# The front of a two-block network kernel: another order of the first weight chunks, a first projection split by features, and late modulation chunks multiplied on GpSimd

## What is computed

```python
mod = jax.nn.silu(c) @ w_ada[l] + b_ada[l]            # 1024 x 6144
mod_c = jax.nn.silu(c_ctx) @ w_ada[l] + b_ada[l]
sh1, sc1, g1, sh2, sc2, g2 = jnp.split(mod[:, None, :], 6, axis=-1)
sh1c, sc1c, g1c, sh2c, sc2c, g2c = jnp.split(mod_c, 6, axis=-1)
hc = modulate(rmsnorm(ctx, norm1_g[l]), sh1c, sc1c)   # h * (1 + scale) + shift
mix_c, ctx_states = token_mixers(hc, *mixer_params, zero_states, not last)
hx = modulate(rmsnorm(x, norm1_g[l]), sh1, sc1)
mix_x, _ = token_mixers(hx, *mixer_params, ctx_states, True)
x = x + g1 * (mix_x @ w_out[l])
x = x + g2 * conv_glu(modulate(rmsnorm(x, norm2_g[l]), sh2, sc2), *ffn_params, True)
...
proj = h @ w_in                                       # first thing in token_mixers
q, k, v, z_g, a_g, b_g, z_s, x_s, B_s, C_s, dt_s = _split(proj, GDN_SPLITS + SSM_SPLITS)
```

## Time and profile before

| | us |
|---|---|
| three timed runs: median | 2697.16 |
| lowest, highest | 2693.72, 2697.79 |
| profiled execution: span from its first to its last instruction | 2695.4 |
| of it PE busy | 2571.0 |
| stages that the change touches: from the start to the first matmul of the mixers | 345.28 |

### The profile page before, as it was taken

How to read it: one execution, slowest core, us unless ns; L and a number is a source line. 1 busy time by engine, 2 the same in 40 slices (tenths; PEclk the granted TensorE clock), 3 DMA queues, 4 the chain that set the end, 5 groups by cost and what they waited for, 6 DMA issues and landing times. The chain is left out here.

```text
span 2695.4 us, 47072 instructions
## 1 busy us (share of the span) xinstructions
PE 2571.0 (95%) x20752; PEld 2004.3 (74%) x20752; DVE 1278.8 (47%) x1994; ACT 510.2 (19%) x1023; POOL 577.4 (21%) x373
## 2 busy tenths in 40 slices
PE   6999889989999999999999999999999999999998
PEld 4555568855888887764888468888878764888886
DVE  2123234554899944642677454442332474445233
ACT  3222123221111101112465110000010261000001
POOL 0000055510000000201222033344333100443332
PEclk9999999999999999999999999999999999999999
DMA  7123100021222123120000012222222101122210
GB/s 302 67 121 156 63 2 3 3 95 63 94 81 76 67 86 129 47 94 32 35 4 4 33 63 94 77 80 94 94 80 94 63 1 63 63 94 94 84 72 32
DMA packets 17370, 195.34 MB, mean 72 GB/s; under 512 B 1896, under 2 KB 3048, under 8 KB 5392
## 3 DMA queue, kind: packets, MB, share of 16 engines
q1 hardware_dynamic: 17168, 192.34, 19.0%
HBM read 190.22 MB, written 2.12 MB: 71 GB/s over the span
## 5 line engine op out<-in xcount | busy, mean ns | idle before, releaser
L3462 PE MATMUL psum<-arena,weight_ring 128*128 128x256 f32 x3072 | 671.2, 379 | 2.9 <-ACT arena L3352 2.9
L3462 PEld LDWEIGHTS psum<-arena,weight_ring 128*128 128x128 f32 x3072 | 582.7, 190 | 85.8 <-ACT arena L3352 5.3
L1862 PE MATMUL psum<-arena,weight_ring 128*128 128x256 f32 x1584 | 349.4, 382 | 5.1 <-DVE arena L2038 4.1
L1862 PEld LDWEIGHTS psum<-arena,weight_ring 128*128 128x128 f32 x1584 | 302.6, 191 | 49.0 <-issue 6.4
L492 PE MATMUL psum<-arena,weight_ring 128*128 128x512 f32 (+1 forms) x672 | 247.3, 526 | 3.6 <-DMA weight_ring<-in_w_in 2.9
L492 PEld LDWEIGHTS psum<-arena,weight_ring 128*128 128x128 f32 x672 | 126.4, 191 | 116.6 <-issue 100.5
L3561 POOL TENSOR_TENSOR weight_ring<-arena,weight_ring 128x1024 f32<-128x1024 f32 x32 | 79.1, 2472 | 380.3 <-PE psum L3462 380.3
L3551 POOL TENSOR_TENSOR arena<-weight_ring 128x1024 f32<-128x1024 f32 x32 | 75.9, 2371 | 287.2 <-POOLq L3245 257.8
L3584 ACT ACTIVATE arena<-psum 128x512 f32<-128x512 f32 (+1 forms) x24 | 12.6, 525 | 620.9 <-PE psum L3462 620.9
L2023 DVE SCALAR_TENSOR_TENSOR arena<-arena,vecs_sb 128x441 f32<-128x441 f32 (+2 forms) x176 | 122.3, 695 | 6.4 <-ACT arena L1938 0.9
L828 DVE SCALAR_TENSOR_TENSOR arena<-psum,vecs_sb,arena 128x511 f32<-128x511 f32 x68 | 40.9, 636 | 163.2 <-ACT arena L705 162.5
(11 more groups left out here) (496 smaller groups left out, 3931.1 us busy)
## 6 DMA issues: line engine op xcount, KB each, us to landing
weight_ring<-in_mlp_up SPq DMA_DIRECT2D x16, 2048.0 KB, 8.0
weight_ring<-in_mlp_down SPq DMA_DIRECT2D x16, 2048.0 KB, 7.9
weight_ring<-in_ada SPq DMA_DIRECT2D x12, 2048.0 KB, 11.8
weight_ring<-in_gate_up SPq DMA_DIRECT2D x11, 2048.0 KB, 8.1
weight_ring<-in_w_in SPq DMA_DIRECT2D x7, 2048.0 KB, 11.6
weight_ring<-in_w_o SPq DMA_DIRECT2D x4, 2048.0 KB, 8.0
weight_ring<-in_w_kv SPq DMA_DIRECT2D x4, 2048.0 KB, 7.9
weight_ring<-in_down_a SPq DMA_DIRECT2D x4, 1536.0 KB, 6.4
```

The costliest lines, as they stand in the source:

```text
L1862: mm = pe.matmul(g.banks[i][:, pair * half:(pair + 1) * half], left[:, j, pair * P:(pair + 1) * P], right(j), start=first and j == 0, stop ...
L3462: mm = pe.matmul(g.banks[i][:, pair * HALF:(pair + 1) * HALF], left[:, j, pair * P:(pair + 1) * P], right(j), start=first and j == 0, stop ...
```

## The change

- `weight_order`: the order becomes ada 0, ada 2, w_in 0, ada 1, ada 3, ada 4, w_in 1, ada 5, w_in 2, ..., ada 9, w_in 6, ada 10, ada 11. Chunk n still lies in slot n % 3.
- `xc` is loaded in two halves, and the first constants stand between the halves.
- `stage_norm1` takes ada 0 and ada 2 alone; the gain is made for features 0 to 511 (`first_gain`), and the stage ends there. The second halves (ada 1, ada 3, copy, turn, bias, gain) stand in `stage_in_proj`. The two idle matmuls at line 300 and the one at line 490 are gone.
- Chunk 0 of w_in: tiles 0, 1 and 2 are taken together, block k by block k, in six banks (`first_products`); ada 1 stands behind k = 1, ada 3 and its turn behind k = 2.
- ada 4 to 11: GpSimd multiplies the chunk in its slot with silu(c) (8 operations of 512 columns), adds the halves (2048 columns, then 1024), and PE sums the remaining two blocks over the partitions with a column of ones: 8 matmuls in place of 32 (`late_sums`, behind tile 1 of chunks 1 to 6; ada 10 and 11 at the end of the stage). Only silu(c) is taken here.
- The last turn and its sum with the bias move to the end of the stage, into bank 7; the sums of the gates move to bank 6.

```diff
-ADAS = ((4,), (5,), (6,), (7,), (8, 9), (10, 11), ())
+LATE_ADAS = ((4,), (5,), (6,), (7,), (8,), (9,), (10, 11))
...
-    order = [("ada", i) for i in range(4)]
-    for i, adas in enumerate(ADAS):
-        order.append(("w_in", i))
+    order = [("ada", 0), ("ada", 2), ("w_in", 0), ("ada", 1), ("ada", 3)]
+    for i, adas in enumerate(LATE_ADAS):
+        if i:
+            order.append(("w_in", i))
         order += [("ada", j) for j in adas]
...
             def _(sp):
                 sp.dma_start(cv[:, :, :], g.t["cc"]).then_inc(s.cond_in, 16)
-                sp.dma_start(xc[:, :, :], g.t["xc"]).then_inc(s.x_in, 16)
-                stream_weights(g, sp, 1, 0)
+                sp.dma_start(xc[:, 0:4, :], g.t["xc"][:, 0:4, :]).then_inc(s.x_in, 16)
                 sp.dma_start(g.consts[:, 0:FIRST_CONSTS], g.t["consts"][:, 0:FIRST_CONSTS]).then_inc(s.consts_in, 16)
+                sp.dma_start(xc[:, 4:8, :], g.t["xc"][:, 4:8, :]).then_inc(s.x_rest, 16)
+                stream_weights(g, sp, 2, 0)
+                sp.dma_start(g.vecs[:, :], g.t["vecs"]).then_inc(s.vecs_in, 16)
                 stream_weights(g, sp, 3, 0)
-                sp.dma_start(g.vecs[:, :], g.t["vecs"]).then_inc(s.vecs_in, 16)
                 sp.dma_start(small[:, :, :], g.t["w_small"]).then_inc(s.small_in, 16)
-                stream_weights(g, sp, 4)
+                stream_weights(g, sp, 5, 0)
...
-                for k in range(KD):
+                for k in range(6):
+                    scaled(k)
+                dve.wait_ge(g.ada_ready, 2)
+                stage_columns(g, dve, 0).then_inc(g.mod_staged, 1)
+                scaled(6)
                 dve.wait_ge(s.vecs_in, 16)
                 dve.wait_ge(g.mod_turned, 1)
...
+                first_gain(g, dve, gain, slice(0, 4), s.gain)
+                scaled(7)
...
+            @block.gpsimd
+            def _(pool):
+                for j in range(4, 12):
+                    c, done = late_ada(j), 10 * (j - 4)
+                    w = g.slots[c % RING][:, :].rearrange("p (k n) -> p k n", k=KD)
+                    pool.wait_ge(g.landed[c % RING], 16 * (c // RING + 1))
+                    for k_ in range(KD):
+                        pool.tensor_scalar(w[:, k_, :], w[:, k_, :], g.cond[:, k_:k_ + 1], None, ALU.mult).then_inc(s.weighed, 1)
+                    pool.wait_ge(s.weighed, done + 8)
+                    pool.tensor_tensor(w[:, 0:4, :], w[:, 0:4, :], w[:, 4:8, :], ALU.add).then_inc(s.weighed, 1)
+                    pool.wait_ge(s.weighed, done + 9)
+                    pool.tensor_tensor(w[:, 0:2, :], w[:, 0:2, :], w[:, 2:4, :], ALU.add).then_inc(s.weighed, 1)
...
+                def first_products(w):
+
+                    for k_ in range(KD):
+                        pe.wait_ge(s.h_done, 2 * (k_ + 1))
+                        for i in range(3):
+                            for off, lo, width in ((0, CTX, SEQ), (1, 0, CTX)):
+                                mm = pe.matmul(g.banks[2 * ((group0 + i) % 3) + off][:, 0:width], w[:, k_, i * P:(i + 1) * P],
+                                               h[:, k_, lo:lo + width], start=(k_ == 0), stop=(k_ == KD - 1))
...
+                        if k_ == 1:
+                            mod_chunk(g, pe, chunk0 + 1, 1, cs)
+                        if k_ == 2:
+                            mod_chunk(g, pe, chunk0 + 2, 3, cs)
+                            pe.wait_ge(g.mod_staged, 2)
+                            mod_turn(g, pe, staged, 0, (1, 3))
+
+                def late_sums(j):
+
+                    if j == 8:
+                        pe.wait_ge(g.mod_staged, 3)
+                    pe.wait_ge(s.weighed, 10 * (j - 3))
+                    w = g.slots[late_ada(j) % RING][:, 0:1024].rearrange("p (k n) -> p k n", k=2)
...
+                            mm = pe.matmul(g.banks[7][32 * q_:32 * q_ + 32, cols], g.c.ones[:, 0:32], w[:, k_, q_ * P:(q_ + 1) * P],
+                                           start=(k_ == 0), stop=(k_ == 1), skip_group_check=True)
+                    mm.then_inc(g.ada_ready, 1)
...
+                        elif m == 1:
+                            late_sums(3 + i)
...
+                            late_sums(10)
+                            late_sums(11)
+                            pe.wait_ge(g.mod_staged, 4)
+                            mod_turn(g, pe, staged, 2)
```

More of the change, by code:

```diff
@@ L256, in stage_norm1 @@
     with ExitStack() as ctx:
-        s = stage_sems(g, ctx, "cond_in", "x_in", "consts_in", "vecs_in", "small_in", "squares", "c_silu", "padded", "sums",
+        s = stage_sems(g, ctx, "cond_in", "x_in", "x_rest", "consts_in", "vecs_in", "small_in", "squares", "c_silu", "padded", "sums",
                        "var", "root", "inv", "spread", "scaled", "mod_sum", "gain")
@@ L297, in _ @@
                 mm.then_inc(s.spread, 1)
-                mod_chunk(g, pe, n_chunk + 2, 2, cs)
-                for _ in range(2):
-                    pe.matmul(g.banks[5][:, :], g.c.ident, g.c.spread, start=True, stop=True)
-                mod_chunk(g, pe, n_chunk + 3, 3, cs)
+                mod_chunk(g, pe, n_chunk + 1, 2, cs)
                 pe.wait_ge(g.mod_staged, 1)
-                mod_turn(g, pe, staged, 0)
+                mod_turn(g, pe, staged, 0, (0, 2))
             @block.scalar
@@ L345, in stage_norm1, with stage_columns, first_gain @@
         g.h = h
-        g.used += 4
+        g.used += 2
+def stage_columns(g, dve, first):
+    both = [ap[:, :].rearrange("p (i t n) -> p i t n", i=2, t=2)[:, :, first, :] for ap in (g.mod_staging, g.banks[7])]
+    return dve.tensor_copy(*both)
+def first_gain(g, dve, gain, ks, done):
+    part = gain[:, ks, :]
+    dve.tensor_scalar(part, g.mod[:, 8 + ks.start:8 + ks.stop, :], 1.0, None, ALU.add).then_inc(done, 1)
+    dve.wait_ge(done, 1)
+    dve.tensor_tensor(part, part, bcast(g.v.norm1_g[:, ks], 2, [P, 4, 2]), ALU.mult).then_inc(done, 1)
 SMALL_AT = 35712 - 256
 CS_AT = SMALL_AT - 32 * KD
-MOD_ROWS_AT = 32512
 GAIN_AT = 33024
@@ L364, in mod_chunk, with mod_bank, mod_turn, mod_rows @@
     mm.then_inc(g.ada_ready, 1)
-def mod_turn(g, pe, staged, part):
-    for i in range(4):
-        mm = pe.transpose(g.banks[6][:, i * P:(i + 1) * P], staged[:, i * P:(i + 1) * P], g.c.ident)
-    mm.then_inc(g.mod_turned, 1)
-def mod_rows(g, part):
-    out = g.mod[:, 16 * part:16 * part + 16, :].rearrange("p (i j) c -> p i j c", j=4)
-    turned = g.banks[6][:, :].rearrange("p (i j r) -> p i j r", i=4, j=4)[:, :, :, 0:2]
-    bias = bcast(g.v.b_ada[:, 16 * part:16 * part + 16].rearrange("p (i j) -> p i j", j=4), 3, [P, 4, 4, 2])
+def mod_bank(g, part):
+    return g.banks[7 if part == 2 else 6]
+def mod_turn(g, pe, staged, part, blocks=range(4)):
+    for i in blocks:
+        mm = pe.transpose(mod_bank(g, part)[:, i * P:(i + 1) * P], staged[:, i * P:(i + 1) * P], g.c.ident)
+    mm.then_inc(g.mod_turned, 1)
+def mod_rows(g, part, blocks=slice(0, 4)):
+    n = len(range(4)[blocks])
+    out = g.mod[:, 16 * part:16 * part + 16, :].rearrange("p (i j) c -> p i j c", j=4)[:, blocks]
+    turned = mod_bank(g, part)[:, :].rearrange("p (i j r) -> p i j r", i=4, j=4)[:, blocks, :, 0:2]
+    bias = bcast(g.v.b_ada[:, 16 * part:16 * part + 16].rearrange("p (i j) -> p i j", j=4)[:, blocks], 3, [P, n, 4, 2])
     return out, turned, bias
@@ L472, in stage_in_proj, with w_in_at, late_ada @@
         chunk0, group0 = g.used, g.groups
+        def w_in_at(i):
+            return chunk0 + (2 + 2 * i if i else 0)
+        def late_ada(j):
+            return chunk0 + (16 if j == 11 else 2 * j - 5)
         with nc.Block() as block:
@@ L487, in product @@
                         for k_ in range(KD):
-                            if i == 0 and off == 0:
-                                if k_ == 0:
-                                    pe.matmul(g.banks[5][:, :], g.c.ident, g.c.spread, start=True, stop=True)
-                                pe.wait_ge(s.h_done, 2 * (k_ + 1))
                             mm = pe.matmul(g.banks[2 * (group % 3) + off][:, 0:width], w[:, k_, (i % 4) * P:(i % 4 + 1) * P],
@@ L634, in _ @@
                 for k_ in range(KD):
+                    if k_ == 4:
+                        act.wait_ge(s.gain, 2)
                     for side, lo, hi in ((1, 0, CTX), (0, CTX, TOK)):
@@ L845, in _ @@
                 inverse_norms()
-                for i in range(5):
-                    unit(i)
-                stage_modulation(12)
-                for i in range(5, len(rows)):
+                for i in range(len(rows)):
                     unit(i)
                 decays()
-                for j in range(10, 13):
+                for j in range(10, len(jobs)):
                     take_turned(j)
-                add_modulation(2)
-                for j in range(13, len(jobs)):
-                    take_turned(j)
+                stage_modulation(12)
                 dve.wait_ge(s.cum_exp, 5)
```

89 lines of the change are left out of this document (48 added, 41 removed).

## The result

The changed kernel takes 2704.51 us (median of 7 runs, 2700.41 to 2707.53) against 2697.69 us before (7 runs, 2693.04 to 2699.14). The ratio is 1.0023, with a 95% interval of 1.0012 to 1.0033: slower by some 6 us. The forecast of 2694 named no change as likeliest, and the time lies 1.5 us above its range.

What follows compares the result with a forecast made beforehand. PE, busy 95% of the 2695.4 us span, was taken as the bound, so time is won where PE waits or sheds work. Terms summed to -3.4 us: span 2692.0, median 2693.8, stated as 2694, range 2686 to 2703.

Steps and rivals of the forecast that it cites:

- End of the stage: From tile 25 to the mixers, with ada 11's load, weighing and late sum: +2.3 us (1.8 to 5).
- GpSimd multiply: Scalar multiply of 512 columns on GpSimd: 0.8 us taken between 522 and 1042 ns, a chunk 13.7 us.
- Rival (c): At the stage's end, waiting for GpSimd's ada 11 makes the kernel slower; 2706.6 us at 2.4 us a multiply, chance 0.08.
- signs of being wrong: w_in 1 issued before 80 us; POOL chunk above 16; PE waiting for later w_in; mixers before 338 or after 348.
- The clock: Low PE clock after idling, at chunk 0's first products and at w_in 1: +1.5 us each.
- the row at 16.34: First modulation chunk, ada 0, on PE: 1.7 us more than a warm one, taken as evidence of low clock.
- the one at 305: Tile at 305.48, clock 0.50 after PE idled: 8.25 us against 7.13, +1.1, taken as evidence of low clock.
- the front: Up to the first product: it begins at 32.0 us, a shift of -8.9 (-9.9 to -8.2).
- the ring: Between chunks 0 and 1: w_in 1 queued behind ada 4 makes PE wait, +11.5 us (11.1 to 12.1).
- the late sums: Cheaper PE sums of the late ada chunks: -3.9 us for ada 5 to 7, then -4.2 and -5.2.
- Rival (b): At w_in 1, PE loses less: -8 (2689 us), or -18 (2679) if issued with the first loads; chance 0.25.
- GpSimd's work for ada 4 to 10: In chunks 1 to 6, weighing at 13.7 us a chunk is ready in time, so PE's late sums never wait.

Runs made afterwards that it cites:

- e2: Changed kernel, but GpSimd only multiplies the last chunk, ada 11, and PE sums its eight blocks; 2701.77 us, ratio 1.0009 to the kernel before.
- f3: Changed kernel's front alone, with ada 4 to 11 taken by PE at the places of the kernel before; 2707.72 us, ratio 1.0037 to that kernel.
- e3: Changed kernel with GpSimd's multiply in another form for each of ada 4 to 7; single run, 2698.50 us.
- h2: Changed kernel plus w_in 1 before ada 4, two-input 512-column multiplies, last sum on PE, two idle matmuls before the first product; 2687.97 us, ratio 0.9956 to before.
- e4: Changed kernel with 14 idle matmuls of 512 columns ahead of PE's wait for w_in 1; single run, 2705.39 us.
- e1: Changed kernel with w_in 1 issued before ada 4 and ada 4's late sum one tile later; 2693.22 us, ratio 0.9975 to the kernel before.
- e1_again: The kernel of e1, unchanged, run once more for its trace; 2688.88 us.

## Why the prediction was wrong, point by point

**The step that failed: "End of the stage".** The forecast was +2.3 us, the trace says +9.5. The term behind it is the GpSimd multiply: bounds of 0.52 and 1.04 us, 0.8 taken, 1.54 measured, outside both. The last chunk took 19.4 us (327.31 to 346.67) where 13.7 were forecast, and PE waited 5.19 us. Behind that wait the late sum and the turn ran at the low clock (1.08 and 1.11 us; at full clock the same 16 records took 0.65, and the turn 0.66 in e2): +0.9. Less the 0.3 us of wait that the forecast had (22.9 against 22.6), that is 5.8 of the 7.2 missed. e2 takes the wait away and wins 4.5 us back. The other 1.3 aren't shown to be the multiply's: tile 24, the first of chunk 6, took 9.59 instead of 8.25 behind PE's wait for DVE at 300.86. Where PE waits 2.7 to 3.5 us there, this tile takes 7.03 (f3) to 9.77 us (e2).

What was wrong in the bounds is the idea that an operation reading one tensor costs no more than one reading two. By the Trainium skill, "GPSIMD Engine Reference", section 4.1, one-input work on GpSimd runs about at line rate and two-input work at half of VectorE's; e3 shows the reverse order, 1.54 and 1.46 against 1.00 us for 512 columns, and the measurement decides. Rival (c) named this place; its threshold of 1.9 us for a multiply, with all else as summed, wasn't reached. At 1.54 the wait alone (5.19, less the 0.3 forecast) turns the sum from -3.4 to +1.5, and what the clock cost beyond its terms does most of the rest. The chance of 0.08 was too low for an operation that no row showed. Two of the prediction's own signs of being wrong came: a POOL chunk above 16 us (19.4) and the mixers beginning after 348 (350.62).

**The clock** was mis-sized in the same direction: +2.5 for the first two blocks of chunk 0 (10.48 against the 7.98 of h2) and +2.1 at w_in 1 (e4 gives 2.0 back), where 1.5 each was taken. The prediction also read the row at 16.34 as low clock. In the window of the earlier trace rows the granted clock is 1.00 there, so of its two rows only the one at 305 shows it, and what made the first chunk take 3.64 us stays open.

**Right:** the front (-9.1), the ring (+11.4; the load landed 12.7 us after its issue, 13.0 were taken), the late sums (-13.1 of -13.3), and that PE waits for no later load of w_in. e1 confirms the mechanism of the ring. It also shows that far more was to be had by it than the gain that it ate: some 15 us. Rival (b) priced that case at -18 against the kernel before; e1's mixers begin 10.1 us sooner than its. Of the 7.9 between, 6.1 are the end of the stage, which e1 leaves as it is (48.2 us from chunk 6 at 287.00 to the mixers, with a wait of 5.13 for GpSimd), and most of the rest is the low clock at the first products.

**Partly right:** GpSimd's work for ada 4 to 10 holds no late sum, as costed, but it is felt elsewhere. DVE's small copies ahead of chunk 6 run beside its multiplies, and PE's wait there is 3.24 us where the kernel before lost 2.74; with two-input operations it is 8.71 to 16.04. No term of the forecast had a price for that.

**Open:** why the mixers take 231.8 us (e4) to 239.9 (e1), with 232.6 before and after the change. In e1 their windows show the clock lower, e1_again shows that it comes back with the same kernel, and nothing here shows which step ahead of them decides it. Nor is it shown why GpSimd's one-tensor form is the slower one.

## What to carry to other kernels

Work that starts sooner is worth what the next load in the same queue allows: read for each load which slot it waits for, and let the one that is needed next go first. An operation that no row of the engine shows needs a bound from rows of the same form or a run of its own, and a wide upper end where its result is waited for. When work goes to an idle GpSimd, look for VectorE copies beside it, and for PE's clock behind every new wait: two idle matmuls took 1.7 us off the first 24 records here.
